# State-space stage: real and imaginary parts side by side along the columns instead of over the two partition halves

## The reference

```python
h = rmsnorm(x, norm_mix[0])                                   # 512 x 1024
a_bar = exp(lam * dt)                                         # complex, 64 groups x 64 states
b_bar = ((a_bar - 1) / lam)[..., None] * complex(b_re, b_im)  # 64 x 64 x 16
bu    = einsum('blgh,gph->blgp', h in 64 groups of 16, b_bar)
state[t] = a_bar * state[t-1] + bu[t]                         # complex, over 512 tokens
y = einsum('blgp,ghp->blgh', state, c).real + d_skip * h
y = gelu(y); val, gate = split(y @ w_glu); x = x + val * sigmoid(gate)
```

## Time and profile before

| | |
|---|---|
| runs of the kernel, median of 3 | 2005.0 us (2003.11 to 2005.42) |
| the profiled execution, its own time | 2000.0 us |
| its span | 1998.2 us |
| mean granted clock of TensorE | 0.968 |
| busy over the span: TensorE, VectorE, ScalarE, GpSimd | 95%, 40%, 41%, 43% |
| state-space stage, until the first product with `w_glu` | 167.7 us |

### The profile page before, as it was taken

How to read it: one execution, slowest core, us unless ns; L and a number is a source line. 1 busy time by engine, 2 the same in 40 slices (tenths; PEclk the granted TensorE clock), 3 DMA queues, 4 the chain that set the end, 5 groups by cost and what they waited for, 6 DMA issues and landing times.

```text
span 1998.2 us, 25979 instructions
## 1 busy us (share of the span) xinstructions
PE 1901.6 (95%) x9160; PEld 1546.0 (77%) x9160; DVE 802.7 (40%) x1402; ACT 826.1 (41%) x1185; POOL 866.4 (43%) x406
## 2 busy tenths in 40 slices
PE   4788999999999999899999999999998999999997
PEld 3677878888887788568888888887885878888886
DVE  8882232222104699844322210355467152222103
ACT  4465444444214433654443331345346244334211
POOL 5753434344444244563444444343434335444441
PEclk7778999999999999899999999999999999999999
DMA  2004322222322122002322322232320213322321
GB/s 108 24 18 164 105 88 97 96 94 94 105 94 95 53 97 94 22 22 75 115 92 97 105 95 94 85 112 77 134 74 11 85 64 107 103 97 92 105 94 42
DMA packets 51808, 171.22 MB, mean 86 GB/s; under 512 B 6689, under 2 KB 11553, under 8 KB 51105
## 3 DMA queue, kind: packets, MB, share of 16 engines
q1 hardware_dynamic: 50304, 165.54, 24.9%
q10 hardware_dynamic: 1440, 4.83, 0.6%
HBM read 165.89 MB, written 2.10 MB: 84 GB/s over the span
## 4 chain that ended last, share of the span: by engine, by line
PE 81%; DVE 11%; DVEq 3%; ACT 2%; issue 2%; SPq 1%; DMA 1%; ACTq 0%
PE ps L228 23%; PE ps L229 23%; PE ps L230 23%; PE ps L1170 2%; DVE score L1699 1%; PE ps L1179 1%; PE ps L1187 1%; PE ps L1443 1%; PE ps L1445 1%; PE ps L1444 1%; DVE h_lo L1079 1%; DVE top L1695 1%; DVE xT L1002 1%; PE ps L717 1%; DVE hsum L1648 0%
## 5 line engine op out<-in xcount | busy, mean ns | idle before, releaser
L218 POOL TENSOR_TENSOR w_lo<-raw,w_hi 128x1024 fp32r<-128x1024 f32 x296 | 713.7, 2419 | 994.5 <-ACT w_hi L211 994.3
L228 PE MATMUL ps<-h_hi,w_hi 128*128 128x512 f32 (+1 forms) x1456 | 572.6, 393 | 7.8 <-DVE h_lo L1079 4.5
L230 PE MATMUL ps<-h_hi,w_lo 128*128 128x512 f32 (+1 forms) x1456 | 569.0, 391 | 0.0
L229 PE MATMUL ps<-h_lo,w_hi 128*128 128x512 f32 (+1 forms) x1456 | 568.8, 391 | 0.0
L211 ACT ACTIVATE w_hi<-raw 128x1024 fp32r<-128x1024 f32 x296 | 311.8, 1057 | 504.5 <-PE ps L230 446.9
L228 PEld LDWEIGHTS ps<-h_hi,w_hi 128*128 128x128 f32 (+1 forms) x1456 | 273.6, 188 | 68.4 <-issue 8.2
L230 PEld LDWEIGHTS ps<-h_hi,w_lo 128*128 128x128 f32 (+1 forms) x1456 | 273.5, 188 | 58.8
L229 PEld LDWEIGHTS ps<-h_lo,w_hi 128*128 128x128 f32 (+1 forms) x1456 | 273.5, 188 | 58.1 <-issue 0.5
L228 PE MATMUL ps<-hid_hi,w_hi 128*128 (+1 forms) x528 | 205.4, 389 | 0.0
L229 PE MATMUL ps<-hid_lo,w_hi 128*128 (+1 forms) x528 | 205.4, 389 | 0.0
L230 PE MATMUL ps<-hid_hi,w_lo 128*128 (+1 forms) x528 | 205.4, 389 | 0.0
(11 more groups left out here) (360 smaller groups left out, 2159.0 us busy)
## 6 DMA issues: line engine op xcount, KB each, us to landing
raw<-in_w_gu SPq DMA_DIRECT2D x132, 512.0 KB, 3.4
raw<-in_w_down SPq DMA_DIRECT2D x66, 512.0 KB, 3.4
raw<-in_w_mix SPq DMA_DIRECT2D x33, 512.0 KB, 3.4
raw<-in_w_dsa SPq DMA_DIRECT2D x29, 512.0 KB, 3.4
raw<-in_w_glu SPq DMA_DIRECT2D x16, 512.0 KB, 3.5
raw<-in_w_out SPq DMA_DIRECT2D x12, 512.0 KB, 3.4
raw<-in_w_o SPq DMA_DIRECT2D x8, 512.0 KB, 3.4
s_x<-in_xs SPq DMA_DIRECT2D x1, 2048.0 KB, 11.2
```

The source lines that it names most:

```text
L218: pool.tensor_tensor(w_lo[slot][:], raw[slot][:], w_hi[slot][:].bitcast(F32), ALU.subtract)\
L228: pe.matmul(o, wh, ah, start=start, stop=False)
L229: pe.matmul(o, wh, al, start=False, stop=False)
L230: return pe.matmul(o, wl, ah, start=False, stop=stop)
```

## The change

Each group's 64 complex states now lie in 64 partitions, with two groups in the two partition halves, and real and imaginary part of a state lie side by side in the columns: where a step had 8 groups in 8 column blocks, it has GP/NQ = QP = 4 pairs of groups, each with a real and an imaginary block. The angles of a step are 128x256 instead of 128x512, and the powers 288 columns instead of 576. In the rotations sine products read the other column block and not the other partition half; the cosine is read twice through a broadcast. The number of columns of z, of the scan and of `winT` stays. On TensorE the products with `win` become 16 with 64 output rows each, the products for `conv` become 4 pairs that sum real and imaginary part over 32 columns, and each of `wout` and `wout_im` is multiplied in two parts on 64 partitions, 16 products of 64x64 each, instead of 8. The sign table is gone; instead a `c_pair` with zeros in it is built in the prologue. All engines' six middle steps are written out, without the loop. The number of output matrices that GpSimd forms, and their size, stays: four instructions of 128x512 in place of two of 128x1024.

```diff
-            with engine.Fori(0, (NQ - 2) // 2) as it:
-                step(it * 2 + 1, 1, it + 1)
-                step(it * 2 + 2, 0, it + 2)
+            for e in range(1, NQ - 1):
+                step(e, e % 2, e // 2 + 1)
...
-        turns = ps[:, ANG_BANK, :].rearrange("p (g c) -> p g c", c=NC)
+        turns = ps[:, ANG_BANK, 0:QP * NC].rearrange("p (g c) -> p g c", c=NC)
...
+            pool.memset(c_pair[:], 0.0)
...
-                pool.tensor_tensor(ang2[p][:], bc(t8_hi[:, gs], 2, NC), bc(const("chunk"), 1, QG), ALU.mult)
+                pool.tensor_tensor(ang2[p][:], bc(t8_hi[:, gs], 2, NC), bc(const("chunk"), 1, QP), ALU.mult)
...
-                pool.tensor_tensor(wout[p][:], bc(pw_re2[:, 1:CH + 1, gs].rearrange("p t g -> p g t"), 3, GH),
-                                   bc(cx[:, gs, :], 2, CH), ALU.mult)
-                pool.tensor_tensor(wout_im[p][:], bc(pw_imn[:, 1:CH + 1, gs].rearrange("p t g -> p g t"), 3, GH),
-                                   bc(cy[:, gs, :], 2, CH), ALU.mult)
+                for o, power, c in ((wout[p][:, 0:QP, :, :], pw_re, c_re), (wout[p][:, QP:QG, :, :], pw_ren, c_im),
+                                    (wout_im[p][:, 0:QP, :, :], pw_imn, c_im), (wout_im[p][:, QP:QG, :, :], pw_imn, c_re)):
+                    pool.tensor_tensor(o, bc(power[:, 1:CH + 1, gs].rearrange("p t g -> p g t"), 3, GH),
+                                       bc(c[:, gs, :], 2, CH), ALU.mult)
...
-            act.activation(cxn[:], craw[:, 0, :], ACT.Copy, scale=const("sign")[:, 1:2])
+            act.wait_ge(S["zeroed"], 2)
+            for n, sign in enumerate((1.0, -1.0)):
+                for half in range(2):
+                    rows = slice(NS * half, NS * (half + 1))
+                    act.activation(c_pair[rows, GP * n:GP * (n + 1), GH * half:GH * (half + 1)],
+                                   craw[rows, n, :].rearrange("p (g h) -> p g h", h=GH), ACT.Copy, scale=sign)
...
-                dve.tensor_tensor(ztmp[0:NS, :, then], z[NS:P, :, now], sin_t[p][NS:P, :, then], ALU.mult)
-                dve.scalar_tensor_tensor(ztmp[NS:P, :, then], z[0:NS, :, now], -1.0, sin_t[p][0:NS, :, then], ALU.mult, ALU.mult)
+                dve.tensor_tensor(ztmp[:, re, then], z[:, im, now], sin, ALU.mult)
+                dve.scalar_tensor_tensor(ztmp[:, im, then], z[:, re, now], -1.0, sin, ALU.mult, ALU.mult)
                 dve.drain()
-                dve.tensor_tensor(z[:, :, now], z[:, :, now], cos_t[p][:, :, then], ALU.mult)
+                dve.tensor_tensor(both(z, now), both(z, now), cos, ALU.mult)
...
-                for g in range(QG):
-                    conv_last = pe.matmul(ps[:, CONV_BANK, g * GH:(g + 1) * GH], winT[:, g, :, :].rearrange("p t h -> p (t h)"),
-                                     cxn[:].rearrange("p (g h) -> p g h", h=GH)[:, bass.ds(e * QG + g, 1), :].rearrange("p a h -> p (a h)"),
-                                     start=True, stop=True)
+                for g in range(QP):
+                    for r in range(2):
+                        conv_last = pe.matmul(ps[:, CONV_BANK, 2 * g * GH:2 * (g + 1) * GH],
+                                              winT[:, QP * r + g, :, :].rearrange("p t h -> p (t h)"),
+                                              c_pair[:, bass.ds(e * QP + (GP * r + g), 1), :].rearrange("p a h -> p (a h)"),
+                                              start=r == 0, stop=r == 1)
...
-                for g in range(QG):
-                    last = pe.matmul(ps[:, Z_BANK[p], g * NC:(g + 1) * NC], win[p][:, g, :],
-                                     xs[:, bass.ds(e * QG + g, 1), :].rearrange("p a c -> p (a c)"), start=True, stop=True)
+                for v in range(QG):
+                    for half in range(2):
+                        rows = slice(NS * half, NS * (half + 1))
+                        last = pe.matmul(ps[rows, Z_BANK[p], v * NC:(v + 1) * NC], win[p][:, v, rows],
+                                         xs[:, bass.ds(e * QG + (QP * half + v % QP), 1), :].rearrange("p a c -> p (a c)"),
+                                         start=True, stop=True)
...
-                for g in SIDES:
-                    pe.matmul(out_of(g), zout[p][:, g, :], wout[p][:, g, :, :], start=False, stop=False)
-                for g in SIDES:
-                    last = pe.matmul(out_of(g), zout[p][:, g, :], wout_im[p][:, g, :, :], start=False, stop=g % 4 == 3)
+                for r in range(2):
+                    for table in (wout[p], wout_im[p]):
+                        for g in SIDES:
+                            rows, v = half_of(g), QP * r + g % QP
+                            last = pe.matmul(out_of(g), zout[p][rows, v, :], table[rows, v, :, :], start=False,
+                                             stop=r == 1 and table is wout_im[p] and g % 4 == 3)
```

More of the change, by code:

```diff
@@ L247, in build @@
         xs = at("s5_x", [G, NC], X)
-        s5_par = at("s5_par", [4, G], RING)
+        s5_par = at("s5_par", [3 * GP + G], RING)
         braw = at("s5_b", [2, G * GH], RING + 1 * KB)
[L250 to L255, removed]
+        craw = at("s5_c", [2, GP * GH], RING + 9 * KB)
+        table_a, table_b = (at(f"s5_table{n}", [CH, NQ, 2, QP], RING + 17 * KB + 2 * KB * n) for n in range(2))
+        ratio_rr, ratio_ii, ratio_ri, ratio_ir = (at(f"s5_part{n}", [CH, GP], RING + 21 * KB + KB * n) for n in range(4))
+        NT9 = (CH + 1) * GP * 4
+        pw = [at(f"s5_pw{n}", [CH + 1, GP], RING + 25 * KB + NT9 * n) for n in range(6)]
+        turn, pw_re, pw_im, pw_ren, pw_imn, wave = pw
+        small = at("s5_small", [16, GP], RING + 25 * KB + NT9 * 6)
         gains = at("s5_gains", [G * GH], RING + 25 * KB + NT9 * 6 + 16 * G * 4)
@@ L276, in build @@
         toep = s5two("s5_toep", [CH, QG, GH])
-        ang2, ang_lo2, ang_sum2 = (s5two(f"s5_ang{n}_", [QG, NC]) for n in range(3))
-        sin_t = s5two("s5_sin", [QG, NC])
-        cos_t = s5two("s5_cos", [QG, NC])
+        ang2, ang_lo2, ang_sum2 = (s5two(f"s5_ang{n}_", [QP, NC]) for n in range(3))
+        sin_t = s5two("s5_sin", [QP, NC])
+        cos_t = s5two("s5_cos", [QP, NC])
         decay = s5two("s5_decay", [QG, NC])
@@ L286, in build @@
         y_q = s5buf("s5_y", [CH, QG * GH // 2])
-        cxn = s5buf("s5_cxn", [G * GH])
+        c_pair = s5buf("s5_c_pair", [2 * GP, 2 * GH])
         sumsq = at("s5_sumsq", [NC], SCR)
@@ L290, in build @@
         xsq = at("s5_xsq", [G, NC], HT + 16 * KB)
-        lam_re, lam_im, log_dt, gain5 = (s5_par[:, n, :] for n in range(4))
+        lam_re, lam_im, log_dt, gain5 = s5_par[:, 0:GP], s5_par[:, GP:2 * GP], s5_par[:, 2 * GP:3 * GP], s5_par[:, 3 * GP:]
         S = {n: sem("s5_" + n) for n in (
@@ L552, in s5_vector @@
             dve.wait_ge(S["wave"], 1)
-            sg = const("sign")
             ai = pw_im[:, 1, :]
@@ L558, in s5_vector @@
             dve.tensor_tensor(pw_re[:], pw_re[:], wave[:], ALU.mult)
-            dve.tensor_scalar(pw_ims, pw_im[:, 0:CH, :], sg[:, 0:1], None, ALU.mult)
             dve.drain().then_inc(S["turn"], 1)
@@ L2431, with halves, by_part @@
     index_w = token_major(w_in[:, 3 * D:3 * D + IH * HD])
-    def states(a):
-        return np.moveaxis(a, 1, 0)
+    def halves(a):
+        return np.moveaxis(a.reshape(NQ, 2, QP, NS, *a.shape[2:]), (1, 3), (0, 1)).reshape(P, GP, *a.shape[2:])
+    def by_part(re, im):
+        re, im = (halves(a).reshape(P, NQ, 1, QP, GH) for a in (re, im))
+        return np.concatenate([re, im], 2).reshape(P, G * GH)
     s5 = {k: i["s5_" + k][0] for k in ("lambda_re", "lambda_im", "log_dt", "b_re", "b_im", "c_re", "c_im", "d", "w_glu")}
-    twice = lambda a, b: np.concatenate([states(a), states(b)], 0)
     gain = np.tile(i["norm_mix"][0].reshape(G, GH).T, (CH, 1))
-    par = np.stack([twice(s5["lambda_re"], s5["lambda_re"]), twice(s5["lambda_im"], s5["lambda_im"]),
-                    np.broadcast_to(s5["log_dt"], (P, G)), gain], 1)
+    par = np.concatenate([halves(s5["lambda_re"]), halves(s5["lambda_im"]),
+                          halves(np.broadcast_to(s5["log_dt"][:, None], (G, NS))), gain], 1)
+    norm = np.broadcast_to(i["norm_mix"][0].reshape(G, 1, GH), (G, NS, GH))
     ct = {k: s5[k].transpose(0, 2, 1) for k in ("c_re", "c_im")}
```

62 lines of the change are left out of this document (36 added, 26 removed).

## The result

The kernel after takes 1984.8 us in the median of its runs (1977.1 to 1986.5), the kernel before on the same chip 2005.2 (2003.1 to 2006.8). The profiled executions lie 16.1 us apart (1983.9 and 2000.0), so my sum of -8.0 is held against -16.1. The profiled execution before is 5 us faster than that kernel's median, so this pair shows less of the change than the medians do.

What follows compares the result with a forecast made beforehand. TensorE bounds the program, which passes stage changes on one for one; VectorE's loop sets full-clock periods. Terms -12.5 (periods), +7 (clock), -6 (prologue), +2.5 (first step), +1 (tail) sum to -8.0: 1997.0 us from 2005.0, range 1986 to 2009.

Steps and rivals of the forecast that it cites:

- VectorE: Stage steps: four angle operations and four sine products at half the columns save 2.1 us, loop 15.1 to 13.0.
- ScalarE: Stage steps: four operations losing 256 columns save 0.85 us; its loop with TensorE's transposes goes from 13.6 to 12.7.
- TensorE: Stage steps: win set 2.0 to 2.2 us, wout set 2.0 to 4.1; full-clock loop 9.8 to 12.1.
- The clock: Six middle periods: two falls to half clock, following transposes and conv, at 3.5 us each: +7.
- First step: Step 0 behind the DMA: the larger wout set at half clock, 3.9 us becoming 6.5: +2.5.
- Prologue: Before toep's first DMA: shorter VectorE work starts token sums at 23.8, 4.75 gained, then 1.1 from angles: -6.
- Tail: Last step: the larger wout set behind VectorE's rotations adds 1 us at full clock, up to 6 at half: +1.
- The loop written out: Six middle steps as straight code: no stall seen at the turn of the loop, so taken as 0.
- rival 3: wout set on TensorE: the new products take turns in the array, 64 costing 6.85 us: +13, 2018 us; chance 0.08.
- Rival 1: Stage: the clock stays full, without the +7 and with 13.0 a period: about -18, 1987 us; chance 0.25.
- Rival 2: Stage: four clock falls in six steps and a slow tail eat all gain: +2.5, 2005 us; chance 0.14.
- Rival 4: Stage: 64x64 products do not lift the clock, TensorE bounds at half clock: +16 or more, 2022 up; chance 0.08.

Runs made afterwards that it cites:

- the fill: Kernel after, plus two unneeded 128x128 by 512-column TensorE products behind each middle step's wout set, into a bank nobody reads: 1977.1 us, ratio 0.987.
- the halves in turn: Kernel after, with the wout products taken as groups 0 to 3, then 4 to 7, instead of alternating partition halves: 1977.5 us, ratio 0.987.

## Why the prediction was right in its direction and short in size

Two terms failed before all others: the price of the win products in halves, put at 2.2 us a step where they took 1.1, and the first step, from which the same set was left out and which so got the wrong sign.

**What bounds the kernel** held. The program behind the stage passed 16.7 us on nearly whole (0.6 lost).

***VectorE*** and ***ScalarE*** held: 0.42 and 0.41 us an operation. At full clock VectorE's 15.1 fell so far that it is level with ScalarE's list and TensorE's transposes: 12.7 and 12.5, where I had 13.0 and 12.7. VectorE's list lost 2.4 us and not 2.1. From start to start the places of the eight halved operations gave 2.8, idle time of 0.4 among it (L641 to L642 was 0.70, L660 to L661 is 0.33, more than the 0.265 I had from the busy times), and the operation on conv behind them took 0.5 back. The run with two more sines and the two with doubled VectorE work show that either list lengthens the step when it grows.

***TensorE*** is the step of the sum that was mis-sized. I priced the win products at 68 ns a record, because L744 costs that with twice the moving columns. They took 34: half the output rows, alternating, and half the columns of L744. So the set went from 2.0 to 1.1 us instead of to 2.2. The wout set took 3.7, not 4.1. TensorE's loop, with 0.74 from y copy to turn, 5.8 from turn to wout, 3.7 and 0.1, is 10.3 us instead of 12.1. I had four loops within 1 us of each other and added 0.2 for their waits; TensorE was in fact out of it by over 2, and a period at full clock was 12.5 to 12.95 instead of 13.2. With six periods at 12.7, the mean that the fill shows, that is -3.0 of what is missing: about half of it is the 0.3 of VectorE's list, the other half the waits that did not come (that they did not because TensorE was out of it is argued).

***The clock*** was near in size and wrong in place. Predicted +7; the kernel with fill shows 5.3 in the periods, and another 2.8 in the tail. But I had put the falls down to the block of transposes and conv. In the kernel with fill that block runs in every step at full clock, and in the kernel after three falls stand behind the idle ends of 2.8 to 3.0 us between the wout set and the transposes of y. Falls within that block do occur in other kernels here (at 69.0 and 113.3 with y copied early, at 71.7 with VectorE's work doubled), so my place for them was possible, and was not this kernel's. I had written that these ends "mostly go"; they stayed, because TensorE got shorter than I thought. The fourth fall, at 138.7, stands in the wait for toep(7)'s DMA, 2.19 us.

***First step***, +2.5 predicted, -1.9 measured, is the one with the wrong sign. I counted the larger wout set and left out the smaller win set in front of it. At half the clock the win set took 1.7 us where the whole-row form takes 1.9 even at full, and the clock rose sooner, within the wout set. The kernel before, written out and with the win halves, shows this part alone, -3.5; what the rest of the change does in the step, above all the larger wout set, gives 1.6 back here and 2.4 to 2.8 in the other profiles of the same first step. This is -4.4 of what is missing, of which up to 1.2 is luck of the profiled execution.

***Prologue***: -7.3, predicted -6. The limit at 23.75 was where I had put it, to 0.05 us. Behind it I had 1.1 less, and it was 2.5 less. That VectorE's list sets the start again when it is made longer is shown by the run that did so, beyond some 2 us that it takes in; that its shortening brought the gain up to the limit fits this and the earlier trace rows.

***Tail***: +2.7, predicted +1; toep(7)'s DMA was waited for, and the wout set behind it ran at half the clock, 5.7 us. Kept at full clock it was -0.1 (9.0 against 9.12).

***The loop written out***: no gain, as taken; the ratio is 1.001 [1.000, 1.003].

So between the sum of -8.0 and the measured -16.1 stand: first step -4.4, full-clock period -3.0, clock in the periods -1.7, prologue -1.3, tail +1.7, rest of the program +0.6. Of the 20 us of medians, 4 more are the profiled execution of the kernel before, which was a fast one; no term of mine stood for them.

**A rule against it.** The Trainium skill (TensorEngine Tiling, Gotcha 1: PSUM Pressure) says that different row tiles cannot access the same PSUM bank simultaneously. The 64 records, which alternate between row halves and write one bank, took 58 ns each where a record alone would be 107 by my estimate from the prologue's sums, so the trace again does not bear it out; and rival 3 (2018 us) fell with it. In the order of four and four, records of the two row halves still interleaved where the groups meet, at 71 ns.

**Rivals.** Rival 1, the clock stays full (1987), came nearest in time, but not by its mechanism: the clock fell four times. Where it really stayed full, in the runs with fill, the kernel takes 1977. Rival 2 had falls that eat everything; they ate 8. Rival 4 fell: the clock rose at 50 us, just as the wout set of 64x64 products began (L778 from 49.99, at 1.09 us for 16), and in the kernel with fill, whose work up to there is the same, it rose at 52.4, within that set:

```profile
50.23 1.97 PE L778 MATMUL ps<-s_wout,s_zout 64*64 64x128 f32 x16
52.00 1.23 PE L778 MATMUL ps<-s_wout_im,s_zout 64*64 64x128 f32 x16
```

**What stays open.** The part of the run-to-run difference (1977.1 to 1986.5 for the kernel after) that is the clock's I can only argue: the mean granted clock of its fastest run was 0.982, of the others 0.976 to 0.978. What exactly brings a fall is open: the falls stand behind idle time of TensorE, but a wait of 2.16 us brought none where one of 1.67 did. The gap of 4 us between medians and profiled pair (20.4 and 16.1) is the fast profiled execution before; how much of it is the clock in the stage and how much the rest of the program no run tells.

The fastest version is the kernel after with two fill products (1977.1), with the halves in turn (1977.5) beside it: both 27 us below the kernel before in their own groups, and some 7.5 below the kernel after by medians, 5 by ratios. The two do not differ by more than the measurement tells.

## What to carry to other kernels

When a change makes several engines faster, price the one that drops out of the race as well: TensorE's shorter list became idle ends, and the clock's falls, three of the four behind such ends, cost 8 us of stage time. Work placed in such an end (two products nobody needs, or a slower order of the same ones) took 6 to 7 us off the stage here and nothing before the change, where the waits stood elsewhere in the step: look first where the idle time ahead of a fall is. Price small matmuls by rows and columns together, and carry a set that gets cheaper through every place where it runs, those at half the clock above all.

## What was not expected of the hardware

- Cutting a set of products in two halves of the output rows, alternating between them, doubles the count and halves the time: 16 records of 125 ns became 32 of 34 ns at full clock, and at half the 32 took 1.7 us.
- Records of different partition halves overlap also when they aren't neighbours in the order: four of one half and four of the other took 71 ns each, alternating ones 58, one alone 107. Where the groups meet their starts stand interleaved in the trace. (The 107 is worked out from products of 512 columns.)
- A wout set 0.8 us longer, and 1.9 us of products added to a step, each made the program 5 to 8 us faster (by ratios and by medians), with a granted clock of 1.00 over 78 us of the stage.
- One and the same list of work takes 2002.3 to 2012.4 us, for the kernel before with its loop written out, and the granted clock tells the two ends apart: 0.967 or 0.968 below 2007, 0.955 to 0.960 above 2009.
